# Late modulation chunks on TensorE: weight blocks stationary and one column moving, in place of a broadcast column and 512 moving

## The chip, the cores and the metric

One core of one Trainium2 chip runs the kernel. The time is the device time of one execution in microseconds (us). All data is fp32.

## The reference, cut to what matters

Two transformer blocks of two layers each work on 256 tokens of width 1024. In the first block each layer is modulated by a vector that depends on the conditioning `c` alone:

```
c_act = jax.nn.silu(c)
for layer in range(DEPTH):
    mod = (c_act @ ada_w[layer] + ada_b[layer])[:, None, :]
    sh1, sc1, g1, sh2, sc2, g2 = jnp.split(mod, 6, axis=-1)
    h = rms_norm(x, norm1_g[layer]) * (1.0 + sc1) + sh1
    x = x + g1 * mixer(h)          # even: retention and local attention; odd: stick-breaking
    h = rms_norm(x, norm2_g[layer]) * (1.0 + sc2) + sh2
    x = x + g2 * grouped_moe(h, ...)
```

`ada_w` is 2 x 1024 x 6144, 50 MB. A vector of 1024 goes against each matrix, so each weight is used once.

## The kernel before, in words

**Chunks.** The modulation is made in 24 chunks `j` of 512 outputs, 12 a layer. With `i = j % 12`, chunks with `i // 2` of 2 or 5 are gates (`g1`, `g2`), which are wanted along a row on all partitions; the others (shifts and scales) are wanted by feature, four columns of 128. In layer 0 chunks 8 and 9 are `sc2`, 10 and 11 are `g2`; in layer 1 chunks 12 and 13 are `sh1`, 14 and 15 `sc1`. Each chunk has two tiles of 1 MB (k blocks 0 to 3 and 4 to 7 of the 1024 rows), each loaded as two transfers of 512 KB.

**The ring.** All weights pass through three slots (`weight_ring`, RING = 3). SyncE issues every load in the order of the plan (`make_plan`; `ada` and `group` on SyncE's queue). Tile n goes into the slot of tile n - 3 and waits until that one is used up: for a tile summed by VectorE until its half is summed (`ada_summed`, `free`, L574 on), for a tile that TensorE reads directly until `weights_used` is raised. So a chunk and a half is all that is loaded ahead.

**Chunks on VectorE.** 21 of 24 chunks are summed by VectorE (`ada_steps`): a scaling by `c_features` of k block 0 (L2335) and seven multiply-adds (L2342), each over 128 x 512, into an accumulator. TensorE then adds over the partitions (`modulate`): four matmuls with 128 columns of the accumulator stationary and one column of ones moving (L858), or for a gate one matmul with ones stationary and 512 columns moving (L855). In the profile each such fp32 matmul is two records. VectorE takes the result (`ada_take`): adds the bias, raises `mod_taken`, and for `i` of 3 or 9 makes gain times scale.

**Chunks on TensorE.** Chunks 10, 12 and 14 (`ADA_ON_PE`) aren't summed by VectorE. TensorE reads the weights themselves (`modulate_a0`, L875): 8 matmuls with one column of `c_features` broadcast to 128 x 128 stationary and 512 weight columns moving, accumulated in one bank, with the same row on all partitions. For chunks 12 and 14, which aren't gates, `ada_take` picks the diagonal blocks out by a multiply with the identity (L2366) and a reduce (L2368).

**Where the chunks stand.** Chunks 0 to 6 are made before and within the input projection of layer 0 (`even_in`). Chunks 7 and 8 are summed within it. Chunks 7 to 15 are handed over within the local attention of layer 0 (`attention(Pairs("a0"))`), which has four items of two heads. TensorE's step t is: score products of item t (L902), values of item t - 2 (L923), fills (`stay_busy`, L739), transposes of the probabilities of item t - 1 (L937), then `in_a0(t)`, where the calls of `modulate_a0(x)` stand. Before the attention it does `modulate_a0(0)` and `(1)`. `modulate_a0(x)` for x of 2 or more waits for `mod_taken` of the chunk two places before, whose bank (6 or 7) it takes. At t of 1 TensorE also waits for `a0_mixed` and transposes the normed retention output (L1235).

VectorE's step t is: reciprocals and scaling of the probabilities of item t - 1 (L2244, L2254), shifted scores of item t (L2263), a copy of the transposed probabilities (L2271), a split of an output (L2275), then its own `in_a0(t)`: at t of 0 the take of x = 2, the reciprocal root, the mixing (L2654, raises `a0_mixed`), and a chunk's sum; at t of 1 and 2 takes and a chunk's sum; at t of 3 and 4 one take. All engines work in program order. The calls before:

```
before t=0: PE chunks 7, 8      DVE sum 9, takes 7, 8
t=0:        PE 9, 10            DVE take 9, mixing, sum 11
t=1:        PE 11, 12           DVE takes 10, 11, sum 13
t=2:        PE 13, 14           DVE takes 12, 13, sum 15
t=3:        PE 15               DVE take 14
t=4:                            DVE take 15
```

Behind the attention TensorE waits for all takes and for the split outputs, and multiplies with `even_out` (L722 to L724), whose weights ScalarE (L1520) and VectorE (L2071) first split into a high and a low part. Then come norm, router (L1078, 16 columns moving), experts, and layer 1, where chunks 16 to 23 are summed by VectorE.

Of the kernel before, what the change touches and what calls it, by code (L numbers as in the profile page):

```python
# [8 lines left out]
ALU = mybir.AluOpType  # L9
# [24 lines left out]
PASSES = GROUPS  # L34

ADA_EVEN, ADA_A0, ADA_ODD, ADA_A1 = (0, 1, 4, 5, 6, 6), 6, 4, 4
ADA_ON_PE = (10, 12, 14)
EVEN_ORDER = [0, 1, 4, 5, 2, 6, 3]
PASS_TILES = 6 * PER_GROUP
EV_ORDER = [3, 4, 5, 0, 1, 2]  # L40
# [63 lines left out]
def make_plan():  # L104

    p = Plan()
    st = {"ada": []}

    def group(name, evac, width=512):

        ts = p.tiles_of(2)
        for t in ts:
            p.tiles[t]["size"] = 4 * width
        st.setdefault(name, []).append((ts, [p.chunk(ts[1], tb == 1, evac) for tb in range(TB)]))

    def proj(name, cols, evac):
        for j in range(-(-cols // 512)):
            group(name, evac, min(512, cols - 512 * j))

    def ada(count):  # L120
        for _ in range(count):
            kind = dict(user="pe", split=False) if len(st["ada"]) in ADA_ON_PE else dict(user="ada")
            st["ada"].append(p.tiles_of(2, **kind))

    def experts(l):
        st[f"moe{l}"] = p.tiles_of(PASSES * PASS_TILES)[0]

    def feed_forward(l):
        st[f"ffn{l}"] = p.tiles_of(3 * FFN_STEPS)[0]
        p.evac["dve"] += 4  # L130

    def cross(l):
        t = p.tile()
        st[f"caq{l}"] = (t, [p.chunk(t, i == 1, "act") for i in range(2)])
        t = p.tile()
        st[f"cao{l}"] = (t, [p.chunk(t, i == 3, "dve") for i in range(4)])

    for l in range(2):
        p.turn(f"mem{l}", KD)
        st[f"kv{l}"] = []  # L140
        for _ in range(2):
            ada(1)
            st[f"kv{l}"].append([p.chunk(None, False, "act") for i in range(2)])
    p.turn("a0h1", KD)
    for j in range(7):
        group("even_in", "act")
        ada(ADA_EVEN.count(j))
    ada(ADA_A0)
    proj("even_out", D, "dve")
    p.turn("a0h2", KD)  # L150
    experts(0)
    p.turn("a1h1", KD)
    for j in range(6):
        group("odd_in", "act")
        if 1 <= j <= ADA_ODD:
            ada(1)
    p.turn("a1qk", 16)
    ada(ADA_A1)
    proj("odd_out", D, "dve")
    p.turn("a1h2", KD)  # L160
    experts(1)
    for j in EV_ORDER:
        if j == EV_ORDER[-1]:
            st["cmp"] = p.tiles_of(2, split=False)
        group("ev_in", "act", min(512, EV_IN - 512 * j))
    p.turn("b0sparse", 8)
    p.turn("b0forget", 8)
    proj("ev_out", D, "dve")
    cross(0)
    feed_forward(0)  # L170
    proj("od_in", OD_IN, "act")
    p.turn("b1q", 8)
    p.turn("b1k", 8)
    proj("od_out", D, "dve")
    cross(1)
    feed_forward(1)
    assert len(st["ada"]) == 24
    return p, st


def build(nc, a, out):
# [3 lines left out]
    with ctx:  # L185
# [85 lines left out]
        PS = ctx.enter_context(nc.psum_tensor("banks", [128, 8, 512], F32))  # L271
        B = [PS[:, i, :] for i in range(8)]

        ADA_ON_DVE = [j for j in range(24) if j not in ADA_ON_PE]

        def ada_sum(j):

# [91 lines left out]
        def slot(n):  # L369
            return W[:, n % RING, :]  # L370
# [175 lines left out]
        def _(eng):  # L546
# [28 lines left out]

            def ada(count=1):
                for _ in range(count):
                    j = loaded_chunks[0]
                    loaded_chunks[0] += 1
                    group(st["ada"][j], a["ada_w"][j // 12], 512 * (j % 12))  # L580

# [118 lines left out]
        def _(eng):  # L700
# [160 lines left out]

            def modulate_a0(x):

                j, bank = 7 + x, 6 + x % 2
                if x >= 2:
                    eng.wait_ge(mod_taken, 7 + x - 1)
                if j not in ADA_ON_PE:
                    modulate(j, bank)
                    return
                for i, t in enumerate(st["ada"][j]):  # L870
                    loaded(t)
                    w = slot(t).rearrange("p (k n) -> p k n", k=4)
                    for k in range(4):
                        at = 4 * i + k
                        mm = eng.matmul(B[bank][:, :], CF[:, at:at + 1].to_broadcast([128, 128]), w[:, k, :],  # L875
                                        start=at == 0, stop=at == KD - 1)
                    mm.then_inc(*used.up())

            normed_n = [0]

# [342 lines left out]
            def in_a0(t):  # L1223

                if t == 0:
                    modulate_a0(2)
                    modulate_a0(3)
                if t == 1:
                    modulate_a0(4)
                    eng.wait_ge(a0_mixed, 1)  # L1230
                    for k in range(RET_HEADS):
                        for tb in range(TB):
# [2 lines left out]
                            mm = eng.transpose(B[2 + k // 2][:, at:at + 128], block, by)  # L1235
                        if k % 2:
                            mm.then_inc(feature_turned, 2)
                    modulate_a0(5)
                    features_wait(RET_HEADS)
                if t == 2:  # L1240
                    modulate_a0(6)
                    modulate_a0(7)
                if t == 3:
                    modulate_a0(8)
            attention(Pairs("a0", P0), in_a0)
            ada[0] += 3 + ADA_A0
            eng.wait_ge(mod_taken, 16)
# [804 lines left out]
        def _(eng):  # L2052
# [292 lines left out]

            ada_taken = [0]

            def ada_take(j, banks, room=None):

                l, i = j // 12, j % 12  # L2350
                if j == 16:
# [7 lines left out]
                if i // 2 in (2, 5):  # L2359
                    g = GB[:, int(i // 2 == 5), (i % 2) * 512:(i % 2 + 1) * 512]  # L2360
                    V(g, bank[:, :], g, ALU.add).then_inc(mod_taken, 1)
                else:
                    new = bank[:, 0:4]
                    if j in ADA_ON_PE:
                        rows = lambda ap: ap.rearrange("p (i f) -> p i f", i=4)
                        V(rows(room), rows(bank), wide(ident.unsqueeze(1), 128, 4, 128), ALU.mult).then_inc(*vec.up())  # L2366
                        settle()
                        eng.tensor_reduce(to, rows(room), AX.X, ALU.add).then_inc(*vec.up())  # L2368
                        settle()
                        new = to  # L2370
                    V(to, new, ABF[:, l, 4 * i:4 * i + 4], ALU.add).then_inc(mod_taken, 1)  # L2371
                if i in (3, 9):
                    n = 2 * l + i // 6
                    eng.wait_ge(mod_taken, ada_taken[0])
# [259 lines left out]
                eng.wait_ge(ret_scores, h + 1)  # L2634
                V(SCR[:, h, :], B[(2, 3, 0, 1)[h]][:, 0:384], SCR[:, h, :], ALU.mult).then_inc(ret_decayed, 1)
            eng.wait_ge(bias_masked, 1)
            room = P0[:, 0, 512:1024]

            def take_a0(x):
                ada_take(7 + x, (6 + x % 2,), room)  # L2640
            ada_steps(KD)
            take_a0(0)
            take_a0(1)

            def in_a0(t):
# [11 lines left out]
                    ins.then_inc(a0_mixed, 1)  # L2657
                    ada_steps(KD)
                if t == 1:
                    take_a0(3)  # L2660
                    for i in range(2):
                        parts[0] += 2
                        eng.wait_ge(features_high, parts[0])
                        hl, hh = [ap[:, 2 * i:2 * i + 2, :].rearrange("p k n -> p (k n)") for ap in (HL, HH)]
                        V(hl, B[2 + i][:, :], hh.bitcast(F32), ALU.subtract).then_inc(features_split, 2)
                    take_a0(4)
                    ada_steps(KD)
                if t == 2:
                    take_a0(5)
                    take_a0(6)  # L2670
                    ada_steps(KD)
                if t == 3:
                    take_a0(7)
                if t == 4:
                    take_a0(8)
            attention(Pairs("a0", P0), (), in_a0)
            splits(at_split[0] + 2)
            add_projected("even_out", 0)
# [425 lines left out]
```

## Time and profile before

| | us |
|---|---|
| median of 3 runs | 1932.01 |
| lowest, highest | 1924.81, 1933.83 |
| profiled execution, its own time | 1938.03 |
| its span | 1936.2 |
| mean granted TensorE clock | 0.962 of 2.4 GHz |

The profile is of one execution; its span runs from the first to the last instruction, and 1.8 us of its own time lie around it. TensorE (PE) has the matmuls, PEld its weight loads, DVE is VectorE, ACT ScalarE, SPq the DMA queue of SyncE. A row of the timeline gives the start, the time from the first start to the last end of a run of like instructions, and in brackets the idle time of the engine before it and what ended it. The clock is given as a share of 2.4 GHz; 0.50 is 1.2 GHz.

### The profile page before, as it was taken

The page shows a single profiled execution, that of the slowest core. Times are in us where ns is not written, and L with a number is a line of the kernel's source. Part 1 is how long each engine was busy: PE and PEld are TensorE (multiplying, and loading weights), DVE is VectorE, ACT ScalarE, POOL GpSimd, SP SyncE. Part 2 cuts the span into 40 slices and gives each one's busy share as a digit, 9 for nine tenths or more (in the row PEclk, how much of TensorE's full clock was granted, in tenths as well). Part 3 has the DMA queues.
Part 4 walks back from the last instruction along what each step waited for, and adds up shares of the span by engine and source line. Part 5 has one row for each costly group of instructions (what it writes and reads, how often), then busy time and mean ns, then how long its engine had stood idle before and what let it go on. Part 6 is the DMA issues. An engine that isn't in the chain of part 4 may idle for free.

```text
span 1936.2 us, 27184 instructions
## 1 busy us (share of the span) xinstructions
PE 1807.3 (93%) x9604; PEld 1494.8 (77%) x9604; DVE 1264.0 (65%) x2000; ACT 1072.8 (55%) x1649; POOL 13.8 (1%) x29
## 2 busy tenths in 40 slices
PE   5998899999999999999999999988999998889998
PEld 4785478888886866888888678676999876669997
DVE  5686658889885766589889652755544565555454
ACT  2443247878873364578878552555444454554443
POOL 1000000000000000000000000000000000000000
PEclk9998889999999999899999998889999999989999
DMA  9866638899993845399899653122656561215652
GB/s 351 298 237 228 202 125 314 323 356 357 322 352 135 314 131 174 120 352 356 324 355 355 224 158 118 44 88 66 186 184 195 166 207 54 88 44 175 194 177 85
DMA packets 217285, 413.09 MB, mean 213 GB/s; under 512 B 13120, under 2 KB 69488, under 8 KB 216800
## 3 DMA queue, kind: packets, MB, share of 16 engines
q1 hardware_dynamic: 214176, 400.74, 60.2%
q0 software_dynamic: 1904, 8.26, 1.3%
q10 hardware_dynamic: 1120, 2.97, 0.4%
q8 instruction: 52, 0.85, 0.2%
q14 instruction: 33, 0.27, 0.0%
HBM read 410.87 MB, written 1.05 MB: 213 GB/s over the span
## 4 chain that ended last, share of the span: by engine, by line
PE 80%; DVE 10%; ACT 5%; issue 2%; DMA 2%; DVEq 0%; ACTq 0%; SPq 0%
PE banks L722 21%; PE banks L724 20%; PE banks L723 20%; PE banks L739 2%; DVE weights_low L2071 2%; PE banks L984 2%; PE banks L1126 2%; DMA weight_ring<-in_ada_w 2%; PE banks L1069 1%; DVE row_gains L2342 1%; PE banks L752 1%; ACT scratch L1671 1%; PE banks L923 1%; PE banks L779 1%; PE banks L875 1%
## 5 line engine op out<-in xcount | busy, mean ns | idle before, releaser
L2071 DVE TENSOR_TENSOR weights_low<-weight_ring,weights_high 128x1024 fp32r<-128x1024 f32 (+1 forms) x656 | 771.8, 1218 | 186.7 <-ACT weights_high L1520 106.5
L722 PE MATMUL banks<-weights_high,features_parts 128*128 128x512 f32 (+1 forms) x1488 | 590.8, 397 | 19.4 <-DVE features_parts L2504 8.2
L724 PE MATMUL banks<-weights_high,features_parts 128*128 128x512 f32 (+1 forms) x1488 | 581.1, 391 | 0.0
L723 PE MATMUL banks<-weights_low,features_parts 128*128 128x512 f32 (+1 forms) x1488 | 581.0, 390 | 0.0
L1800 ACT ACTIVATE weights_high<-weight_ring 128x1024 fp32r<-128x1024 f32 x384 | 391.1, 1055 | 102.4 <-PE banks L724 72.7
L722 PEld LDWEIGHTS banks<-weights_high,features_parts 128*128 128x128 f32 x1488 | 281.3, 189 | 84.4 <-DVE weights_low L2071 16.3
L724 PEld LDWEIGHTS banks<-weights_high,features_parts 128*128 128x128 f32 x1488 | 280.9, 189 | 59.4
L723 PEld LDWEIGHTS banks<-weights_low,features_parts 128*128 128x128 f32 x1488 | 281.2, 189 | 55.4 <-issue 1.0
L1520 ACT ACTIVATE weights_high<-weight_ring 128x1024 fp32r<-128x1024 f32 (+1 forms) x176 | 176.0, 1043 | 139.3 <-PE banks L724 85.5
L722 PE MATMUL banks<-features_parts,weights_high 128*128 128x256 f32 x736 | 210.5, 286 | 1.1 <-DVE features_parts L2166 1.0
L723 PE MATMUL banks<-features_parts,weights_high 128*128 128x256 f32 x736 | 208.4, 283 | 0.0
L724 PE MATMUL banks<-features_parts,weights_low 128*128 128x256 f32 x736 | 208.4, 283 | 0.0
L722 PEld LDWEIGHTS banks<-features_parts,weights_high 128*128 128x128 f32 x736 | 141.3, 192 | 3.2 <-issue 1.7
L723 PEld LDWEIGHTS banks<-features_parts,weights_high 128*128 128x128 f32 x736 | 141.5, 192 | 0.7
L724 PEld LDWEIGHTS banks<-features_parts,weights_low 128*128 128x128 f32 x736 | 141.3, 192 | 0.0
L2016 ACT ACTIVATE weights_high<-weight_ring 128x1024 fp32r<-128x1024 f32 x96 | 96.0, 1048 | 55.8 <-PE banks L724 55.8
L739 PE MATMUL banks<-fill 128*128 128x512 f32 x406 | 124.0, 450 | 0.3 <-DVE modulation L2371 0.3
L2342 DVE SCALAR_TENSOR_TENSOR row_gains<-weight_ring,c_features,row_gains 128x512 f32<-128x512 f32 x133 | 99.9, 751 | 28.6 <-DMA weight_ring<-in_ada_w 20.8
L739 PEld LDWEIGHTS banks<-fill 128*128 128x128 f32 x406 | 82.9, 214 | 23.7 <-issue 8.1
L2903 DVE TENSOR_TENSOR projected<-projected,banks 128x256 f32<-128x256 f32 x44 | 18.5, 421 | 104.6 <-PE banks L724 104.6
L1671 ACT ACTIVATE scratch<-scratch,row_shifts 128x128 f32<-128x128 f32 (+1 forms) x80 | 36.2, 454 | 71.6 <-DVE row_shifts L2263 71.6
L1993 ACT ACTIVATE features_parts<-projected 128x512 fp32r<-128x512 f32 x22 | 13.9, 630 | 74.7 <-PE banks L724 74.7
(371 smaller groups left out, 1620.2 us busy)
## 6 DMA issues: line engine op xcount, KB each, us to landing
weight_ring<-in_exp_w_gate SPq DMA_DIRECT2D x128, 512.0 KB, 5.0
weight_ring<-in_exp_w_up SPq DMA_DIRECT2D x128, 512.0 KB, 5.0
weight_ring<-in_exp_w_down SPq DMA_DIRECT2D x128, 512.0 KB, 5.1
weight_ring<-in_ada_w SPq DMA_DIRECT2D x96, 512.0 KB, 5.6
weight_ring<-in_ffn_wg SPq DMA_DIRECT2D x44, 512.0 KB, 4.1
weight_ring<-in_ffn_wu SPq DMA_DIRECT2D x44, 512.0 KB, 4.7
weight_ring<-in_ffn_wd SPq DMA_DIRECT2D x44, 512.0 KB, 4.2
weight_ring<-in_even_w_in SPq DMA_DIRECT2D x28, 512.0 KB, 5.7
```

Source lines behind the costliest of these rows:

```text
L722: eng.matmul(dst, lh, rh, start=first, stop=False, **kw)
L723: eng.matmul(dst, lh, rl, start=False, stop=False, **kw)
L724: mm = eng.matmul(dst, ll, rh, start=False, stop=last, **kw)
L739: eng.matmul(B[bank][:, :], FILL[:, :], FILL[:, :].unsqueeze(1).to_broadcast([128, 4, 128]), start=True, stop=True, skip_group_check=True)
L984: mm = eng.matmul(B[4 + b][:, k * 128:(k + 1) * 128], NB[:, tb, (4 * b + k) * 128:(4 * b + k + 1) * 128], SEL[:, tb, :], start=(tb == 0), ...
L1126: mm = eng.matmul(B[4 + q % 4][:, 0:256], left, right, start=i == 0, stop=i == len(steps) - 1)
L1520: eng.activation(half_of(high(s), i, t["size"]), half_of(slot(t["n"]), i, t["size"]), ACT.Copy)\
L1671: eng.activation(p, p, ACT.Exp, scale=-1.0, bias=small(SHIFT, t)[:, i:i + 1], accum_out=small(SUMS, t)[:, i:i + 1]).then_inc(probs_ready, 1)
L1800: eng.activation(half_of(high(t["split"]), x), half_of(slot(t["n"]), x), ACT.Copy)\
L2016: eng.activation(half_of(high(t["split"]), x), half_of(slot(t["n"]), x), ACT.Copy)\
L2071: V(half_of(low(s), i, size), half_of(slot(n), i, size), half_of(high(s), i, size).bitcast(F32), ALU.subtract)\
L2342: ins = eng.scalar_tensor_tensor(out=acc, in0=w, scalar=CF[:, k:k + 1], in1=acc, op0=ALU.mult, op1=ALU.add)
```

## The change

Of chunks 7 to 15, TensorE now makes 9, 12, 13, 14 and 15 from the weights, none of them a gate; the gates 10 and 11 are summed by VectorE. TensorE's form is turned round: a block of 128 x 128 weights is stationary and one column of `c_features` moves, 32 matmuls a chunk (for each of four blocks of outputs, eight of k), and the result stands by feature in four columns. TensorE waits for both tiles before the first matmul, and the first tile is given back only four matmuls (eight records) before the last (`i == 3`, `k == 3`), the second at the last. Chunk 12 is loaded ahead of 11 (`ADA_LOADS`). `ada_take` needs no identity and no reduce. The calls of both engines move:

```
before t=0: PE chunks 7, 8      DVE takes 7, 8
t=0:        PE 9                DVE take 9, mixing, sum 10
t=1:        PE 10, 12           DVE take 10, sum 11
t=2:        PE 11, 13           DVE takes 12, 11
t=3:        PE 14               DVE take 13
t=4:        PE 15               DVE take 14
t=5:                            DVE take 15
```

The diff, cut to its core:

```diff
-ADA_ON_PE = (10, 12, 14)
+ADA_ON_PE = (9, 12, 13, 14, 15)
+ADA_LOADS = [*range(11), 12, 11, *range(13, 24)]
+A0_CHUNKS = [7, 8, *ADA_LOADS[9:16]]
...
     def ada(count):
         for _ in range(count):
-            kind = dict(user="pe", split=False) if len(st["ada"]) in ADA_ON_PE else dict(user="ada")
-            st["ada"].append(p.tiles_of(2, **kind))
+            j = ADA_LOADS[len(st["ada"])]
+            kind = dict(user="pe", split=False) if j in ADA_ON_PE else dict(user="ada")
+            st["ada"][j] = p.tiles_of(2, **kind)
...
             def modulate_a0(x):
 
-                j, bank = 7 + x, 6 + x % 2
+                j, bank = A0_CHUNKS[x], 6 + x % 2
...
-                for i, t in enumerate(st["ada"][j]):
+                for t in st["ada"][j]:
                     loaded(t)
-                    w = slot(t).rearrange("p (k n) -> p k n", k=4)
-                    for k in range(4):
-                        at = 4 * i + k
-                        mm = eng.matmul(B[bank][:, :], CF[:, at:at + 1].to_broadcast([128, 128]), w[:, k, :],
-                                        start=at == 0, stop=at == KD - 1)
-                    mm.then_inc(*used.up())
+                for i in range(4):
+                    for k in range(KD):
+                        w = slot(st["ada"][j][k // 4]).rearrange("p (k n) -> p k n", k=4)[:, k % 4]
+                        mm = eng.matmul(B[bank][:, i:i + 1], w[:, i * 128:(i + 1) * 128], CF[:, k:k + 1],
+                                        start=k == 0, stop=k == KD - 1)
+                        if i == 3 and k % 4 == 3:
+                            mm.then_inc(*used.up())
...
                 if t == 0:
                     modulate_a0(2)
-                    modulate_a0(3)
                 if t == 1:
-                    modulate_a0(4)
                     eng.wait_ge(a0_mixed, 1)
...
-                    modulate_a0(5)
+                    modulate_a0(3)
+                    modulate_a0(4)
                     features_wait(RET_HEADS)
                 if t == 2:
+                    modulate_a0(5)
                     modulate_a0(6)
-                    modulate_a0(7)
-                if t == 3:
-                    modulate_a0(8)
+                if t in (3, 4):
+                    modulate_a0(t + 4)
...
-                    new = bank[:, 0:4]
-                    if j in ADA_ON_PE:
-                        rows = lambda ap: ap.rearrange("p (i f) -> p i f", i=4)
-                        V(rows(room), rows(bank), wide(ident.unsqueeze(1), 128, 4, 128), ALU.mult).then_inc(*vec.up())
-                        settle()
-                        eng.tensor_reduce(to, rows(room), AX.X, ALU.add).then_inc(*vec.up())
-                        settle()
-                        new = to
-                    V(to, new, ABF[:, l, 4 * i:4 * i + 4], ALU.add).then_inc(mod_taken, 1)
+                    V(to, bank[:, 0:4], ABF[:, l, 4 * i:4 * i + 4], ALU.add).then_inc(mod_taken, 1)
...
-            ada_steps(KD)
             take_a0(0)
             take_a0(1)
...
                 if t == 1:
-                    take_a0(3)
...
-                    take_a0(4)
+                    take_a0(3)
                     ada_steps(KD)
                 if t == 2:
+                    take_a0(4)
                     take_a0(5)
-                    take_a0(6)
-                    ada_steps(KD)
-                if t == 3:
-                    take_a0(7)
-                if t == 4:
-                    take_a0(8)
+                if 3 <= t <= 5:
+                    take_a0(t + 3)
```

## Rows read from the trace of the kernel before

**Rows 1.** The page: busy time, clock in 40 slices, the chain that ended last.

```profile
PE 1807.3 (93%) x9604; PEld 1494.8 (77%) x9604; DVE 1264.0 (65%) x2000; ACT 1072.8 (55%) x1649; POOL 13.8 (1%) x29
...
PEclk9998889999999999899999998889999999989999
...
PE 80%; DVE 10%; ACT 5%; issue 2%; DMA 2%; DVEq 0%; ACTq 0%; SPq 0%
```

**Rows 2.** Waits from 110 to 260 us: total, times, longest (us).

```profile
ACT scratch L1671 <- DVE row_shifts L2263: 45.0, 4, 15.1
...
DVE row_gains L2342 <- DMA weight_ring<-in_ada_w: 12.4, 4, 4.9
```

**Rows 3.** Timeline of TensorE, 155 to 236 us: start, duration (us), instruction, idle before.

```profile
164.78 1.84 PE L858 MATMUL banks<-constants,row_gains 128*128 128x1 f32 x16
166.56 0.93 PE L902 MATMUL banks<-qk_features 64*128 64x128 f32 x8
172.22 1.84 PE L858 MATMUL banks<-constants,row_gains 128*128 128x1 f32 x8 [4.73 <-DVE modulation L2371]
173.92 10.03 PE L875 MATMUL banks<-weight_ring,c_features 128*128 128x512 f32 x16
...
188.39 1.54 PE L937 MATMUL banks<-constants,scratch 128*128 128x128 f32 x6 [3.59 <-DVE scratch L2254]
189.73 1.92 PE L855 MATMUL banks<-row_gains,constants 128*128 128x512 f32 x2
191.44 1.91 PE L1235 MATMUL banks<-constants,normed 128*128 128x128 f32 x8
193.14 7.19 PE L875 MATMUL banks<-weight_ring,c_features 128*128 128x512 f32 x16
...
205.17 1.00 PE L937 MATMUL banks<-constants,scratch 128*128 128x128 f32 x6 [2.29 <-DVE scratch L2254]
...
208.72 9.71 PE L875 MATMUL banks<-weight_ring,c_features 128*128 128x512 f32 x16 [1.76 <-DVE modulation L2371]
...
227.14 1.65 PE L739 MATMUL banks<-fill 128*128 128x512 f32 x3
...
231.14 1.55 PE L923 MATMUL banks<-scratch,projected 128*64 128x256 f32 x8 [1.07 <-DVE features_parts L2275]
232.62 2.94 PE L739 MATMUL banks<-fill 128*128 128x512 f32 x8
```

**Rows 4.** Stretches: us; busy by engine (instructions); clock; DMA share; GB/s.

```profile
168.00:172.00 4.00, 0.00 (x0) 0.00 (x0) 3.69 (x6) 1.04 (x1) 0.00 (x0) 0.69 0.77 217
194.00:197.00 3.00, 3.00 (x8) 1.33 (x7) 2.71 (x5) 0.04 (x1) 0.00 (x0) 1.00 0.03 6
266.00:268.00 2.00, 1.60 (x15) 1.63 (x15) 0.25 (x1) 1.34 (x2) 0.00 (x0) 1.00 0.00 0
270.00:272.00 2.00, 2.00 (x11) 2.00 (x11) 0.00 (x0) 0.00 (x0) 0.00 (x0) 0.50 0.00 0
```

**Rows 5.** Timeline of VectorE in the same stage.

```profile
165.87 0.49 DVE L2335 TENSOR_SCALAR row_gains<-weight_ring,c_features 128x512 f32<-128x512 f32 x1 [8.51 <-PE banks L858]
166.39 5.68 DVE L2342 SCALAR_TENSOR_TENSOR row_gains<-weight_ring,c_features,row_gains 128x512 f32<-128x512 f32 x7
...
174.61 2.16 DVE L2654 SCALAR_TENSOR_TENSOR normed<-banks,reciprocal_root,projected 128x128 f32<-128x128 f32 x8
...
184.48 3.18 DVE L2342 SCALAR_TENSOR_TENSOR row_gains<-weight_ring,c_features,row_gains 128x512 f32<-128x512 f32 x4 [4.89 <-DMA weight_ring<-in_ada_w]
...
207.78 0.69 DVE L2368 TENSOR_REDUCE modulation<-projected 128x4 f32<-128x512 f32 x1
```

**Rows 6.** Timeline of TensorE at the router's products, 253 to 292 us.

```profile
266.40 1.93 PE L1078 MATMUL banks<-router_w,qk_features 128*128 128x16 f32 x16 [0.73 <-DVE qk_features L2105]
...
269.71 3.43 PE L1078 MATMUL banks<-router_w,qk_features 128*128 128x16 f32 x16
```

**Rows 7.** Timeline of the DMA issues on SyncE's queue, 180 to 183 us.

```profile
180.55 0.88 SPq L563 DMA_DIRECT2D weight_ring<-in_ada_w  x2
```

More of the change, by code:

```diff
@@ L106, in make_plan @@
     p = Plan()
-    st = {"ada": []}
+    st = {"ada": {}}
     def group(name, evac, width=512):
@@ L272, in build @@
         B = [PS[:, i, :] for i in range(8)]
-        ADA_ON_DVE = [j for j in range(24) if j not in ADA_ON_PE]
+        ADA_ON_DVE = [j for j in ADA_LOADS if j not in ADA_ON_PE]
         def ada_sum(j):
@@ L577, in ada @@
                 for _ in range(count):
-                    j = loaded_chunks[0]
+                    j = ADA_LOADS[loaded_chunks[0]]
                     loaded_chunks[0] += 1
@@ L2346, in _, with ada_take @@
             ada_taken = [0]
-            def ada_take(j, banks, room=None):
+            def ada_take(j, banks):
                 l, i = j // 12, j % 12
@@ L2636, in _ @@
             eng.wait_ge(bias_masked, 1)
-            room = P0[:, 0, 512:1024]
             def take_a0(x):
-                ada_take(7 + x, (6 + x % 2,), room)
-            ada_steps(KD)
+                ada_take(A0_CHUNKS[x], (6 + x % 2,))
             take_a0(0)
```

## The prediction

> **What bounds the kernel now.** I read the page first: TensorE is busy 93% of the span at a granted clock mostly of 2.4 GHz, and the chain that ended last lies on it for 80% [rows 1]. That average hides the stage of the change, the local attention of layer 0 (165 to 236 us), so I then read the waits of that stretch. ScalarE's exponentials wait 45.0 us in four waits on VectorE, and VectorE's chunk sums wait 12.4 us for transfers [rows 2]. The timeline of TensorE shows the stage as a chain in program order: score products, transposes of the last item, chunks between them, with TensorE idle before several pieces [rows 3]. So the end of the stage is set by TensorE and VectorE in turn. Whatever stands between two items on TensorE is on the path; its gaps (4.73, 3.59, 2.29, 1.76 us) are what could cover new work. The clock matters here as nowhere else: 0.69 of full over 168 to 172 us, 1.00 at 194 to 197 [rows 4].
>
> **What the change removes.** VectorE sums 19 chunks and not 21. In the stage it summed 9, 11, 13 and 15; now 10 and 11. A chunk is one scaling and seven multiply-adds, 0.49 + 5.68, back to back 6.1 us [rows 5], so 12.3 us go. The multiply by the identity and the reduce of the old TensorE chunks 12 and 14 (the reduce alone 0.69 us, twice) go too [rows 5]. TensorE loses three chunks of 16 records of 512 columns: 10.03, 7.19 and 9.71 us, 27 us in all [rows 3]; also three small column sums (1.84 us at the low clock, about 0.95 at the high).
>
> **What it adds.** Five chunks, each of 32 fp32 matmuls. The column sum L858 is the same form (128x128 stationary, one column moving); its 16 records stand for 8 matmuls, so a chunk is 64 records. Price at 2.4 GHz: 16 records took 1.84 us [rows 3], 0.106 each, 6.9 us a chunk. Price at 1.2 GHz: eight records at 172.22 took 1.84 us, 0.213 each, 13.8 us a chunk. No row shows 64 in a run, so these are the two ends. The old chunk took 7.2 us at the high clock, so at the high clock a chunk costs what it did, and at the low clock a third more than the 10.03 of the slowest old one.
>
> **Which end.** The router's products are the nearest row: 16 columns moving, 32 records in two groups of 16 [rows 6]. The first 16 took 1.93 us; the clock fell with TensorE hardly idle (1.60 us busy in 266 to 268, then 2.00 in 270 to 272 at 0.50), and the next 16 took 3.43 us [rows 4, 6]. Half the records at each price gives 32 x 0.106 + 32 x 0.213 = 10.2, with the last one's end 10.3 us a chunk. I take that for the four chunks that follow dense work (transposes, fills, scores), which raised the clock before them: at 194 to 197 it was back at 1.00 after the 128- and 512-column work from 188.39 on [rows 3, 4].
>
> The Trainium skill, "TensorE: Matmul & The Clock Gate", section "Why this matters for your kernels", says to keep TensorE continuously busy and free of long idle gaps, and the clock stays released. Taken by itself that would give the new chunks the 2.4 GHz price, since they leave no gap, and the first rival's time below. The router rows speak against it.
>
> **The sum along the path**, in the profile's own times.
> - Chunk 9. TensorE needn't wait for VectorE's sum of it (the 4.73 us idle before 172.22 goes), and starts at 167.4. Until then it does what it did, so the clock falls at about 169.5 as before [rows 4]: 20 records at 0.106, 44 at 0.213, end 179.1.
> - VectorE takes it only then, and the mixing (2.16 us [rows 5]) stands behind that take: 181.8. Chunk 10's sum, 6.1 us, to 188.0; its second tile lands before it is wanted (its slot is free at 177.4, and 3.9 us pass from issue to use, as from 180.55 to 184.48 [rows 5, 7]). The transposes start at 188.8, not 188.39: +0.4. So what VectorE gains by not summing chunk 9 is spent waiting for it.
> - Transposes, normed transposes and chunk 10's ones-matmul, issued 1.3 + 1.7 + 1.7 us [rows 3], to 193.6. Chunk 12: 203.9 (its old end was 200.3): +3.6.
> - The second tile of chunk 11 is behind chunk 12 in the ring: its slot comes free 8 records before the end of chunk 12, at 202.2, lands at 206.1, four steps take 3.2 us (as from 184.48) and scaling 0.9: transposes at 210.2, not 205.17: +5.0. The reorder 12, 11 doesn't remove this wait, it makes it hang on a longer chunk.
> - 1.4 + 1.7 us, then chunk 13: 223.6. Its old counterpart, chunk 14, ended at 218.4: +5.2.
> - From here VectorE sums nothing and the old waits are gone, but TensorE is back to back: scores 1.8, values 1.5, fills 1.6, transposes 1.4 (low-clock rows [rows 3]; scores twice their 0.93) to 229.9; chunk 14 to 240.2; 4.5 us more to 244.7; chunk 15 to 255.0. Then the last values, which stood at 231.14.
>
> That is **+23.9 us**. The transfers of 14, 15 and of the second tile of even_out come free at 221.9, 238.5 and 253.3 and land 3.9 us later, before 229.9, 244.7 and the 259 at which ScalarE reaches that tile: hidden by 4.1, 2.3 and about 1.5 us; without that cover each costs its lateness. The swap of loads 11 and 12, the new bank order and the extra step of takes cost nothing besides: the moved instructions (0.15 to 0.7 us) lie in VectorE's waits. Behind the last values nothing changes: fills, splits and even_out follow as from 232.62 on.
>
> The profiled execution's time is 1938.0 us (span 1936.2), 6.0 above the median 1932.0 of the runs. 1938.0 + 23.9 = 1961.9; on the median, 1932.0 + 24 = **1956 us**.
>
> **Rivals.**
> 1. *The high clock holds* (not slower). Chunk 9 ends at 174.3, VectorE's chunk 10 at 183.1, transposes 183.9; chunk 12 at 193.4; chunk 11's late tile lands 196.5, transposes 200.6; chunks 13, 14, 15 end at 209.2, 219.7 and 230.1, the last two each after 3.9 us for a tile behind the chunk before. Last values at 230.1 and not 231.14: -1 us, 1931. It decides if a chunk runs at 0.106 throughout. For it: L858 in pairs at the high clock. Against: the router's records. Chance 0.12, with anything up to +9.
> 2. *The low clock throughout.* Four chunks at 13.8 and not 10.3 add 14 us: +38, 1970. For it: the clock stayed low through L858 and the first matmuls after it (172.22 to 178). Against: 5 to 6 us of dense work between chunks. A tile landing late adds to it. Chance 0.17 for +31 and more.
> 3. *VectorE was the bound and TensorE's gaps take the work.* At the high clock five chunks are 34.5 us against 21.6 + 2.9 before, 10 us more, while the five gaps of [rows 3] hold 13.4, and the old chunks' low-clock share (27 - 21.6 = 5 us) is saved: -11, 1921. Against: gaps aren't where the chunks stand; VectorE now waits for chunk 9, and two late tiles remain. Chance 0.05.
>
> **Chances and range.** The forecast's own case, a chunk of 9.5 to 11.7 us, holds +20 to +31 us, 1952 to 1963, with 0.62; 0.04 lies between it and the first rival. A measurement can tell some 0.5%, 9.7 us, from no change: faster 0.05, same 0.12, slower 0.83. The range 1944 to 1969 leaves out the first and third rival and the worst of the second.
>
> **What would show it.** Right: the new chunk matmuls with 64 records each, single records spaced 0.106 in a first part and 0.213 after; the clock at 0.50 for most of 170 to 255 us, with the low digit in two more slices of the page; VectorE idle 5 us or more before the take of chunk 9, and again for chunk 11's second tile; the last values near 255; everything behind shifted alike. Wrong: clock at 1.00 in the middle of a chunk's second half (first rival); no gap on VectorE before the mixing; a TensorE wait for a tile above 1 us; or a shift that shrinks after even_out.

## The result, and the profile after

The changed kernel takes 1959.2 us in the median of 4 runs (1952.2 to 1963.5), the kernel before 1930.1 in the same comparison: ratio 1.0142, 95% interval [1.0112, 1.0172]. A second comparison of the unedited changed kernel (6 runs, below) gave 1.0168 [1.0143, 1.0193]. The profiled execution took 1963.5 us, with a span of 1961.8.

Three lines of the page, against [rows 1]: TensorE is busier by 32 us, its clock shows 7 and 5 tenths in the fourth and fifth slice, where 8 and 8 stood before, and it holds one more per cent of the chain.

```profile
PE 1839.2 (94%) x9854; PEld 1542.0 (79%) x9854; DVE 1251.0 (64%) x1980; ACT 1074.0 (55%) x1649; POOL 13.8 (1%) x29
...
PEclk9997589999999999899999998798999998989999
...
PE 81%; DVE 9%; ACT 5%; issue 2%; DMA 1%; SPq 0%; DVEq 0%; ACTq 0%
```

The timeline of TensorE in the stage, against [rows 3]. L878 is the new chunk line, L906 the scores, L927 the values, L941 the transposes, L742 the fills; the five rows of L878 are chunks 9, 12, 13, 14 and 15.

```profile
164.54 0.93 PE L906 MATMUL banks<-qk_features 64*128 64x128 f32 x8
165.40 11.54 PE L878 MATMUL banks<-c_features,weight_ring 128*128 128x1 f32 x64
...
186.48 1.54 PE L941 MATMUL banks<-constants,scratch 128*128 128x128 f32 x6 [7.97 <-DVE scratch L2257]
...
191.23 10.55 PE L878 MATMUL banks<-c_features,weight_ring 128*128 128x1 f32 x64
...
208.07 1.06 PE L941 MATMUL banks<-constants,scratch 128*128 128x128 f32 x6 [2.04 <-DVE scratch L2257]
...
211.82 13.79 PE L878 MATMUL banks<-c_features,weight_ring 128*128 128x1 f32 x64 [0.98 <-DMA weight_ring<-in_ada_w]
...
230.39 11.47 PE L878 MATMUL banks<-c_features,weight_ring 128*128 128x1 f32 x64
...
245.98 10.55 PE L878 MATMUL banks<-c_features,weight_ring 128*128 128x1 f32 x64
256.46 1.55 PE L927 MATMUL banks<-scratch,projected 128*64 128x256 f32 x8
```

Both stages are best measured from the start of the first score products to the start of the last values: 64.6 us before (166.56 to 231.14), 91.9 now (164.54 to 256.46), **27.3 us more**. In front of it this execution was 2.0 us earlier, behind it both take the same, 1705.1 and 1705.3 us to the end of the span: 27.3 - 2.0 + 0.3 is the span's 25.6. So between these two executions the stage is the whole difference.

The new chunks take 11.54, 10.55, 13.79, 11.47 and 10.55 us, 57.9 in all. The clock over six stretches (columns as in [rows 4]): in chunks 12 and 14 it is high in the first microseconds and low in the rest, in chunk 13 low from the start, while TensorE is busy without a gap.

```profile
192.00:195.00 3.00, 3.00 (x29) 3.00 (x29) 2.81 (x5) 0.00 (x0) 0.00 (x0) 1.00 0.00 0
196.00:201.00 5.00, 5.00 (x26) 5.00 (x25) 0.00 (x0) 0.00 (x0) 0.00 (x0) 0.50 0.00 0
...
206.00:208.00 2.00, 0.04 (x1) 0.00 (x0) 1.93 (x6) 0.00 (x0) 0.00 (x0) 1.00 1.02 368
...
212.00:225.00 13.00, 13.00 (x62) 13.00 (x63) 0.70 (x3) 0.00 (x0) 0.00 (x0) 0.50 0.10 36
231.00:233.00 2.00, 2.00 (x20) 2.00 (x19) 1.64 (x8) 0.03 (x1) 0.00 (x0) 0.95 0.44 164
234.00:241.00 7.00, 7.00 (x34) 7.00 (x34) 0.00 (x0) 0.00 (x0) 0.00 (x0) 0.50 0.00 0
```

Single records of chunk 9 in two stretches, 165 to 167 us and 170 to 176 us (duration in ns, least/median/most):

```profile
L878 PE MATMUL banks<-c_features,weight_ring x15: 250/250/271, 165.4 to 167.0; 128*128 128x1 f32 x15
```

```profile
L878 PE MATMUL banks<-c_features,weight_ring x30: 352/352/352, 169.8 to 175.9; 128*128 128x1 f32 x30
```

15 records start within 1.6 us at the high clock and 30 within 6.1 us at the low: 0.11 us apart, and 0.21.

VectorE, against [rows 5], now waits where it worked before: 10.27 us for chunk 9, 9.17 us for the second tile of chunk 11, 14.52 us for scores behind chunk 13.

```profile
176.97 0.16 DVE L2366 TENSOR_TENSOR modulation<-banks,ada_bias_features 128x4 f32<-128x4 f32 x1 [10.27 <-PE banks L878]
...
204.16 3.18 DVE L2345 SCALAR_TENSOR_TENSOR row_gains<-weight_ring,c_features,row_gains 128x512 f32<-128x512 f32 x4 [9.17 <-DMA weight_ring<-in_ada_w]
...
227.22 0.29 DVE L2266 CUSTOM_DVE_ANT_0 scratch<-banks,aux 128x128 f32<-128x128 f32 x1 [14.52 <-PE banks L906]
```

### The profile page after: what moved, and what is told of

Its sections match the earlier page's. It is cut to its first block, busy times and chain, and to the rows that moved or that the text cites. A ratio compares the mean times of both kernels' runs of the same rounds, so it can differ in the third digit from the quotient of the medians.

```text
span 1961.8 us, 27659 instructions
## 1 busy us (share of the span) xinstructions
PE 1839.2 (94%) x9854; PEld 1542.0 (79%) x9854; DVE 1251.0 (64%) x1980; ACT 1074.0 (55%) x1649; POOL 13.8 (1%) x29
## 4 chain that ended last, share of the span: by engine, by line
PE 81%; DVE 9%; ACT 5%; issue 2%; DMA 1%; SPq 0%; DVEq 0%; ACTq 0%
PE banks L725 21%; PE banks L727 20%; PE banks L726 20%; PE banks L878 3%; DVE weights_low L2074 2%; PE banks L742 2%; PE banks L988 2%; PE banks L1130 1%; PE banks L1073 1%; DMA weight_ring<-in_ada_w 1%; DVE row_gains L2345 1%; PE banks L755 1%; PE banks L782 1%; PE banks L906 1%; PE banks L927 1%
## 5 line engine op out<-in xcount | busy, mean ns | idle before, releaser
L742 PE MATMUL banks<-fill 128*128 128x512 f32 x406 | 121.6, 444 | 0.3 <-DVE modulation L2366 0.3
L2345 DVE SCALAR_TENSOR_TENSOR row_gains<-weight_ring,c_features,row_gains 128x512 f32<-128x512 f32 x119 | 89.4, 751 | 24.8 <-DMA weight_ring<-in_ada_w 17.5
L742 PEld LDWEIGHTS banks<-fill 128*128 128x128 f32 x406 | 81.7, 211 | 23.4 <-issue 8.0
L878 PEld LDWEIGHTS banks<-c_features,weight_ring 128*128 128x128 f32 x320 | 58.1, 286 | 3.9 <-DVE row_gains L2364 2.5
```

The costliest lines, as they stand in the source:

```text
L742: eng.matmul(B[bank][:, :], FILL[:, :], FILL[:, :].unsqueeze(1).to_broadcast([128, 4, 128]), start=True, stop=True, skip_group_check=True)
L878: mm = eng.matmul(B[bank][:, i:i + 1], w[:, i * 128:(i + 1) * 128], CF[:, k:k + 1], start=k == 0, stop=k == KD - 1)
L2345: ins = eng.scalar_tensor_tensor(out=acc, in0=w, scalar=CF[:, k:k + 1], in1=acc, op0=ALU.mult, op1=ALU.add)
```

## The experiments

Ratios are to the kernel before, run on the same chip. "Stage" is the time from the first scores to the last values in the one profiled execution of each version, and line numbers shift by a few from version to version. The rest of the kernel is the same in all versions, yet from the last values to the end of the span the profiled executions took from 1690 to 1708 us, and the stage of one and the same version moved by 3.8 us (run 10). So neither a span nor a few microseconds of one stage tell versions apart by themselves.

Where the rest differs, the traces show. From 940 to 1100 us behind the last values the clock was 0.82 to 0.85 in the five executions whose rest took 1704 to 1708 us (before, changed, runs 4, 8 and 10), 0.91 to 0.94 in the six with 1690 to 1694 (runs 1, 2, 5, 6, 7 and 9), and 0.88 in run 3 with 1698. The changed kernel, then run 6, over the same stretch:

```profile
1196.00:1356.00 160.00, 145.43 (x804) 112.65 (x803) 84.78 (x290) 72.38 (x201) 0.00 (x0) 0.82 0.24 79
```

```profile
1196.00:1356.00 160.00, 140.31 (x863) 107.94 (x862) 93.13 (x313) 81.16 (x226) 0.00 (x0) 0.94 0.25 80
```

Between the same two groups of transposes (L782) around that stretch, at 1138.03 and 1323.99 us in the changed kernel and at 1135.59 and 1311.36 in run 6, lie 186.0 and 175.8 us: 10 of the 13.7 us by which these two rests differ. So some 10 us of a median's difference can come from far behind the stage. Whether a version sets them or chance does, no run here shows.

**1. The same records, with 128 columns moving.** Only the moving column is repeated; the four results stand 128 columns apart.

```diff
-mm = eng.matmul(B[bank][:, i:i + 1], w[:, i * 128:(i + 1) * 128], CF[:, k:k + 1], ...)
+mm = eng.matmul(B[bank][:, i * 128:(i + 1) * 128], w[:, i * 128:(i + 1) * 128],
+                CF[:, k:k + 1].to_broadcast([128, 128]), ...)
...
-V(to, bank[:, 0:4], ABF[:, l, 4 * i:4 * i + 4], ALU.add)
+new = bank[:, 0:512:128] if j in ADA_ON_PE else bank[:, 0:4]
+V(to, new, ABF[:, l, 4 * i:4 * i + 4], ALU.add)
```

> The changed kernel, but the moving column of c_features is broadcast to 128 columns, so each of the 64 records of a chunk streams 128 columns (the normed transposes, of that width, stand 0.106 apart at 2.4 GHz and 0.213 at 1.2). Same results, same records, same weights loaded, same order; only the array is fed for the whole record. Theory (the clock falls because the matmuls are narrow): records 0.107 us apart, a chunk 6.9 us after the clock is back, clock at 1.00 through chunks 13 to 15, last values 20 to 26 us earlier than in the changed kernel; 1930 to 1938 us, ratio to the kernel before 1.000 to 1.004. Rival (64 weight loads, or the order of the chunks and their waits, set the loss, whatever the clock): chunks stay at 10.5 to 13.8 us, ratio 1.012 to 1.017.

Measured: ratio 1.0041 [1.0015, 1.0067], stage 72.8 us. Timeline of TensorE, then the clock over the last three chunks:

```profile
166.51 0.93 PE L906 MATMUL banks<-qk_features 64*128 64x128 f32 x8
167.36 7.41 PE L878 MATMUL banks<-c_features,weight_ring 128*128 128x128 f32 x64
...
189.07 7.95 PE L878 MATMUL banks<-c_features,weight_ring 128*128 128x128 f32 x64
...
203.88 1.42 PE L941 MATMUL banks<-constants,scratch 128*128 128x128 f32 x6 [4.31 <-DVE scratch L2257]
...
208.31 7.38 PE L878 MATMUL banks<-c_features,weight_ring 128*128 128x128 f32 x64 [1.30 <-DMA weight_ring<-in_ada_w]
...
220.31 7.38 PE L878 MATMUL banks<-c_features,weight_ring 128*128 128x128 f32 x64 [1.41 <-DMA weight_ring<-in_ada_w]
...
239.28 0.87 PE L927 MATMUL banks<-scratch,projected 128*64 128x256 f32 x8
```

```profile
208.00:240.00 32.00, 28.35 (x242) 26.05 (x242) 5.73 (x26) 3.27 (x12) 0.00 (x0) 1.00 0.42 145
```

The same 64 weight loads and 64 matmuls, each with 128 times the columns, take 7.4 us (chunk 12, which began at the low clock, 7.95) and not 10.5 to 13.8, and the clock stays at 1.00 through chunks 13 to 15. The stage loses 19.1 us of the 27.3, a little under the 20 to 26 expected, and the ratio is just above its range. The rival (weight loads, order, waits at whatever clock) falls. The chunk is 0.5 us longer than I expected, and the 8.2 us left are not the clock's in the main. Run 3, below, has the same order and a stage 8.0 us shorter: 4.0 us of that are waits (here 4.31 us before the second transposes, 203.88, and 1.30, 1.41 and 1.93 us for late tiles), 2.2 us the chunks' own time.

**2. The new form alone.** The kernel before, with the new form in chunks 12 and 14 and no pick by VectorE; all else as before.

```diff
+if j != 10:
+    ...                      # the 32 matmuls with one column moving
+    return
```

> The kernel before with the new form for chunks 12 and 14 alone (chunk 10, a gate, keeps its form; allocation, load order and calls are those of before). Theory (clock): chunk 12 takes 10.3 instead of 7.2 us, chunk 14 10.3 to 13.8 instead of 9.7, both on the path, less 1.4 us for the pick that goes from VectorE once before a wait of TensorE: +3 to +6 us, ratio 1.0015 to 1.003. Rival (the loss comes from the allocation and the order, not from the form): -1 to -3 us.

Measured: ratio 1.0054 [1.0034, 1.0074], stage 78.7 us (+14.1). Timeline of TensorE, the two chunks between first scores and last values:

```profile
163.12 0.93 PE L913 MATMUL banks<-qk_features 64*128 64x128 f32 x8
...
188.73 13.78 PE L876 MATMUL banks<-c_features,weight_ring 128*128 128x1 f32 x64 [0.16 <-DMA weight_ring<-in_ada_w]
...
213.60 13.78 PE L876 MATMUL banks<-c_features,weight_ring 128*128 128x1 f32 x64 [2.79 <-DMA weight_ring<-in_ada_w]
...
241.84 0.87 PE L934 MATMUL banks<-scratch,projected 128*64 128x256 f32 x8 [1.07 <-DVE features_parts L2286]
```

The sign is the theory's, the size above it: both chunks ran at the low clock from end to end, 13.78 us each, where 7.19 and 9.71 stood, and chunk 14 waited 2.79 us for its tile. Two such chunks in the old order already cost 8.8 us between the medians, where 3 to 6 were expected.

**3. The new allocation and order alone**, with the old form and VectorE's picks for all five chunks.

```diff
 ADA_ON_PE = (9, 12, 13, 14, 15)
...
-    (32 matmuls, one column moving)
+    (8 matmuls, one column broadcast and stationary, 512 moving; identity and reduce in ada_take)
```

> The changed kernel's allocation, load order and calls, with the old form of the TensorE chunks (one broadcast column stationary, 512 columns moving, and VectorE picking the diagonals). Theory (clock): each of the five chunks takes 7.2 us at the high clock and 10 to 13 at the low, which lasts only until the first dense stretch is over, so 7.2 to 10 each; against the changed kernel 5 x 2 to 3 us less, against the one before +8 to +15 us, ratio 1.004 to 1.008. Rival (the loss is in the number of chunks on TensorE, whatever the form): ratio 1.012 to 1.016.

Measured: ratio 1.0022 [0.9994, 1.0051], stage 64.8 us, against 64.6 before. Timeline of TensorE:

```profile
163.33 0.93 PE L905 MATMUL banks<-qk_features 64*128 64x128 f32 x8
...
186.77 7.03 PE L878 MATMUL banks<-weight_ring,c_features 128*128 128x512 f32 x16
...
198.19 1.00 PE L940 MATMUL banks<-constants,scratch 128*128 128x128 f32 x6 [1.84 <-DVE scratch L2256]
...
228.09 0.87 PE L926 MATMUL banks<-scratch,projected 128*64 128x256 f32 x8
```

My expectation was too high: the chunks took 7.03 to 7.13 us, all at the high clock, and their first tile comes back at half, so the second transposes waited only 1.84 us (198.19). Five chunks on TensorE and the new order cost nothing measurable. **The form is the loss, not the allocation.** Run 2 has the new form without the new allocation and order and is slower; run 3 has these without the form and isn't. To the form belongs here, beside the one moving column, that both tiles are awaited first and the first is given back late.

**4. 64 columns moving.** Run 1 with half the width; the four results stand 64 columns apart.

```diff
-CF[:, k:k + 1].to_broadcast([128, 128])
+CF[:, k:k + 1].to_broadcast([128, 64])
```

> As the run with 128 broadcast columns, with 64: the array is fed for half of each record. Theory (clock, by how wide the matmuls are): between the changed kernel and the run with 128 columns, the clock at 1.00 for more of the stage than with one column; ratio 1.002 to 1.012. If the clock acted on or off by the mere presence of one-column matmuls it would equal the run with 128 columns. Rival (weight loads): ratio 1.012 to 1.017 as changed.

Measured: ratio 1.0111 [1.0055, 1.0166] from 4 runs, stage 75.2 us. Timeline of TensorE, and the clock over chunk 14:

```profile
168.83 0.93 PE L906 MATMUL banks<-qk_features 64*128 64x128 f32 x8
...
208.90 7.39 PE L878 MATMUL banks<-c_features,weight_ring 128*128 128x64 f32 x64
...
220.87 12.16 PE L878 MATMUL banks<-c_features,weight_ring 128*128 128x64 f32 x64 [1.37 <-DMA weight_ring<-in_ada_w]
...
243.98 0.87 PE L927 MATMUL banks<-scratch,projected 128*64 128x256 f32 x8
```

```profile
221.00:232.00 11.00, 11.00 (x61) 11.00 (x61) 0.62 (x3) 0.00 (x0) 0.00 (x0) 0.58 0.16 60
```

Four of the chunks took 7.3 to 7.6 us, chunk 14 12.16, since the clock fell early within it (0.58 over 221 to 232). The stage lies between one column (91.9) and 128 (72.8). The runs of this version spread from 1937 to 1964 us, so the ratio says little more than that. No other width was tried.

**5. The first tile given back at half a chunk.** The first tile's k blocks for all four output blocks, then the second tile's. Each output block still opened its own accumulation, and the kernel's results came out wrong (run 9 has them right); instructions and transfers are as many as in the changed kernel, so the times can be compared.

```diff
-for i in range(4):
-    for k in range(KD):
+for h in range(2):
+    for i in range(4):
+        for k in range(4 * h, 4 * h + 4):
             ...
+    mm.then_inc(*used.up())
```

> The changed kernel with the 64 records of a chunk in another order: the first tile's four k blocks for all four output blocks, then the second tile's. The first tile is given back after half the chunk and not 8 records before its end. Theory (the late tile of chunk 11 is a second, small loss): it comes 24 records earlier, 5.1 us at the low clock, so TensorE's 2.04 us before the transposes and 0.98 us before chunk 13 go: 3 us less than the changed kernel, ratio 1.012 to 1.013; the chunks' own 10.5 to 13.8 us stay. Rival (tiles are the main loss, not the clock): 10 us less or more, ratio under 1.009.

Measured: ratio 1.0130 [1.0102, 1.0158], stage 89.9 us, 2.0 less than the changed kernel. Timeline of TensorE:

```profile
167.27 0.93 PE L906 MATMUL banks<-qk_features 64*128 64x128 f32 x8
...
208.61 0.82 PE L941 MATMUL banks<-constants,scratch 128*128 128x128 f32 x6
...
213.68 12.66 PE L879 MATMUL banks<-c_features,weight_ring 128*128 128x1 f32 x64 [3.39 <-DMA weight_ring<-in_ada_w]
...
257.17 1.55 PE L927 MATMUL banks<-scratch,projected 128*64 128x256 f32 x8
```

The 2.04 us before the second transposes are gone (208.61 follows the fills), but chunk 13's own second tile is late by 3.39 us in their place, where it was 0.98. So the waits together are no shorter, and of the 2.0 us 1.4 are the chunks' own (56.5 us in all, not 57.9), which move by more than that between executions of one version (run 10). The early return alone has no gain that can be told; the rival (10 us) falls.

**6. VectorE takes chunk 9 later**, behind the mixing and the sum of chunk 10.

```diff
 if t == 0:
-    take_a0(2)
     root(8)
     ...
     ada_steps(KD)
+    take_a0(2)
```

> The changed kernel, but VectorE takes chunk 9 behind the mixing and the sum of chunk 10, not ahead of them. Theory: mixing and the first tile's steps go into the 10.3 us in which VectorE waited for chunk 9; the second tile of chunk 10 (issued 176.0, lands 180) and its four steps then set the transposes at 184 and not 186.5: 2.5 us less than the changed kernel, ratio 1.0125 to 1.0135. Rival (VectorE isn't on the path there): no difference.

Measured: ratio 1.0095 [1.0069, 1.0120], stage 90.2 us, 1.7 less than the changed kernel. Timeline of VectorE at chunk 10's second tile:

```profile
181.35 1.54 DVE L2345 SCALAR_TENSOR_TENSOR row_gains<-weight_ring,c_features,row_gains 128x512 f32<-128x512 f32 x2 [8.53 <-DMA weight_ring<-in_ada_w]
```

VectorE is on the path there: TensorE's idle time before the first transposes is 4.99 us and not 7.97. VectorE now waits for the tile that TensorE's chunk 9 holds. Chunk 9 took 12.89 us in this execution and not 11.54, so its tile came back 1.35 us later; that covers the 0.8 us missing from the 2.5 expected. The 1.7 us by themselves lie within what one version's stage moves by; run 8 against run 3 tests the same edit with chunks whose times hardly change. The ratio is lower than the stage explains: against the 1.0142 and 1.0168 of the changed kernel it says 9 to 14 us. The difference lies behind the stage: the rest took 1691.6 us here and 1705.3 and 1703.6 in the two profiles of the changed kernel, at the clocks shown above. Why stays open.

**7. All three together**: 128 columns, first tile back at half, later take. The results are wrong as in run 5, the instructions the same in number and size.

> The changed kernel with the 128 broadcast columns, the first tile given back at half, and the take of chunk 9 behind the sum of chunk 10. Theory: the three losses are the clock, the late tiles and the take, and they are all of it. Against the run with 128 columns alone: transposes of item 0 5.4 us earlier, 3.1 of the 4.3 us before the next ones gone, and the 1.30, 1.41 and 1.93 us for tiles gone, so the last values come 59 us after the first scores (before 64.6, changed 91.9): 1924 to 1926 us, ratio 0.996 to 0.999. Rival (something else holds the stage): ratio 1.001 to 1.004.

Measured: ratio 0.9946 [0.9927, 0.9966], stage 60.1 us, 31.8 less than the changed kernel: the three losses together are more than the 27.3 us, and nothing else holds the stage. The ratio is below its range of 0.996 to 0.999. It says 10 us against the kernel before, the stage 4.5; the rest took 1692.0 us here and 1705.1 in the profile of before.

**8. The old form in the new order, with the later take.**

> The allocation and order of the changed kernel with the old form (512 columns moving), and the take of chunk 9 behind the sum of chunk 10. Theory: as the run of that order with the old form, whose last values came 64.8 us after the first scores, less the 5.8 us by which the mixing and the sum of chunk 10 come earlier: 59 us, ratio 0.997 to 1.000. Rival: no difference from the old form in that order, 1.002.

Measured: ratio 0.9966 [0.9946, 0.9987], stage 60.2 us, 4.6 less than run 3. The chunks took 7.03 to 7.18 us in both runs, and TensorE's idle time before the first transposes went from 10.13 to 5.21 us, so these 4.6 us are the later take's. The ratio is just below its range. It is faster than the kernel before, by 0.3%; its rest (1705.2 us) was as long as that of before (1705.1), and the stage is 4.4 us shorter.

**9. Run 7 with one opening a chunk.**

```diff
-start=k == 0, stop=k == KD - 1, skip_group_check=True)
+start=h == i == k == 0, stop=k == KD - 1, skip_group_check=True)
```

> As the run with 128 columns, the first tile given back at half and the later take, but only the first matmul of a chunk opens an accumulation, not the first of each of the four output blocks. With four openings the first tile's share was lost from the sums. Theory: an opening clears the accumulate marks of the whole bank, so the three later openings made the second tile's matmuls overwrite what the first had left in the blocks before; with one opening nothing is lost. The instructions are the same in number and size, so the time is that of the run with four: last values 60 us after the first scores, 1922 us, ratio 0.993 to 0.997. Rival (the loss of the sums has another cause, or an opening costs time): sums still off, or another time.

Measured: the sums are whole; ratio 0.9976 [0.9954, 0.9998], stage 62.7 us. Timeline of TensorE:

```profile
165.24 0.93 PE L906 MATMUL banks<-qk_features 64*128 64x128 f32 x8
...
178.45 1.40 PE L941 MATMUL banks<-constants,scratch 128*128 128x128 f32 x6 [4.08 <-DVE scratch L2257]
...
199.18 8.98 PE L879 MATMUL banks<-c_features,weight_ring 128*128 128x128 f32 x64 [0.75 <-DVE row_gains L2364]
...
227.95 0.87 PE L927 MATMUL banks<-scratch,projected 128*64 128x256 f32 x8
```

The time is 2.6 us longer in the stage than run 7's, of which chunk 13 is 1.6 (8.98 and not 7.38 us: it began at the low clock, 0.50 over 199 to 201). That is within what the stage moves by between executions. The ratio is a little above its range; it is under 1 by hardly more than its interval, and the stage is 1.9 us shorter than before. Between runs 7, 8 and 9 the intervals overlap; I would take run 8, whose chunks are the shorter.

**10. The changed kernel again.**

> The changed kernel itself, unedited, against the kernel before, beside the version above on the same chip. Theory: the stage takes 90 to 93 us from the first scores to the last values against 64.6, so +26 to +28 us; ratio 1.012 to 1.016. If the later take and the early return of tiles (each 1.7 to 2.0 us shorter in the stage, but 1.0095 and 1.0130 as ratios) had gained more than their stages show, it stays at 1.014; if those ratios scatter by what the rest of the kernel does, it may come out lower, at 1.010 to 1.013.

Measured: ratio 1.0168 [1.0143, 1.0193], just above the range; stage 95.7 us, also above it. Timeline of TensorE:

```profile
212.74 12.85 PE L878 MATMUL banks<-c_features,weight_ring 128*128 128x1 f32 x64 [2.47 <-DMA weight_ring<-in_ada_w]
```

Chunks 12.71, 11.40, 12.85, 10.77 and 13.65 us: the last one never saw the high clock for long. The same program's stage differs by 3.8 us between the two profiled executions, and 3.5 of these are the chunks', by where in each the clock falls. The wait for chunk 13's tile was 2.47 us here and 0.98 there.

## Why the prediction was right

It forecast 1956 us with a range of 1944 to 1969, slower; 1959.2 was measured. The case that came true is the forecast's own, +20 to +31 us, but at its upper end: the medians lie 29.1 us apart and not 24, and part of the nearness is that the kernel before came out at 1930.1, 2 us under the median it was added to. In run 10 the ratio says 32 us, in the second rival's band. Step by step, with the execution's times moved by the 2.0 us by which its first scores came earlier:

- *Chunk 9* was to end at 179.1 and ended at 179.0; *the transposes of item 0* 188.8 and 188.5; *chunk 12* 203.9 and 203.8; *the transposes of item 1*, behind the late tile, 210.2 and 210.1. So for these steps the two prices per record (0.106 and 0.213), the shares at either (20 and 44 records in chunk 9, half and half in chunk 12), the take of chunk 9 ahead of the mixing, and the ring's wait behind chunk 12 are right to 0.3 us. That is of this execution: in run 10 chunk 9 took 12.71 us and chunk 12 11.40, each about 1 us more.
- *Chunk 13* was to end at 223.6 and ended at 227.6. Here the size is off by 4.0 us: the middle price of 10.3 us was taken for every chunk that follows dense work, and this one took 13.79, the low price. The clock had risen by 206 (1.00 in the stretch 206 to 208) but TensorE stood idle for 2.04 us there and again for 0.98 us, and it was down again before the chunk. Those 0.98 us, for the chunk's own second tile, the sum had at nothing; a tile wait above 1 us was among its signs of being wrong, and in run 10 this one was 2.47 us. It is the second rival's price in one of four chunks, and in run 10 chunk 15 took nearly that price too (13.65). Over both profiled executions the eight chunks behind dense work average 11.9 us, so the middle price was too low, not only unlucky once.
- *Chunks 14 and 15* took 11.47 and 10.55 us, and from the end of 13 to the last values I had 31.4 and measured 30.9. That is in part luck: the two chunks were together 1.4 us longer than twice 10.3, and the work before them 1.9 us shorter than its low-clock prices (4.8 and 4.1 us, not 6.3 and 4.5), the first mostly since the clock rose there (L742 1.30 us, L941 0.82). The sum came to +23.9, the stage to +27.3: the 3.4 us are chunk 13's.
- *What VectorE sheds* buys nothing: VectorE does 12.3 us less of sums and stands in the waits of 10.27, 9.17 and 14.52 us shown above. That the first of them was on the path, run 6 and run 8 against run 3 show; for the others it is read from the timeline.
- *The reason for the low clock.* The router's records were the evidence, and run 1 is the test: equal records with wider moving operand, 19 us back. The first rival needed the high clock all through a chunk of one-column matmuls; none of the ten such chunks profiled in the two executions of the changed kernel had it (10.55 us was the shortest, 6.9 its price). The Trainium skill, "TensorE: Matmul & The Clock Gate", section "Why this matters for your kernels", advises keeping TensorE continuously busy. By this case that isn't enough: 13.00 of 13 us busy over 212 to 225 at a clock of 0.50, and 28.35 of 32 us busy at 1.00 with 128 columns. The measurement decides.
- *The third rival* (VectorE was the bound, 1921 us) was wrong for this change. Its own terms (10 us more, less 13.4 and 5) come to some -8 us, not the -11 that it states. Runs 7 and 8, at 1922 and 1924 us, are near its number, but their stages are 4.5 and 4.4 us shorter than before, not 11. So much the gaps could take once the chunks ran at the high clock and VectorE no longer waited for chunk 9.

What I expected wrongly in the experiments was twice the same thing: the chance share of the low clock, taken as a middle price where an execution has one end or the other (runs 2 and 3). Beside these, the ratios of runs 1, 7, 8, 9 and 10 lay outside their ranges by 0.0001 to 0.0014, that of run 6 by 0.003; that is no more than the stage and the rest move by between executions.

## What to carry to other kernels

Don't price a long run of narrow matmuls at the high clock: with one column moving, the weights stationary and TensorE always busy, 64 records took 10.5 to 13.8 us here, and with 128 equal columns mostly 7.4. The added columns cost some 0.5 us a chunk against the 6.9 that one column would take at the high clock, and over the last three chunks the clock stood at 1.00. And a take that waits for a long chunk belongs behind everything on its engine that doesn't need it: that was worth 4.6 us in the stage (run 8 against run 3). Before a few microseconds are put down to a change, look where in the trace two executions differ.

## What the runs showed of the hardware that was not expected

- A wider moving operand made the same work faster: 7.4 us against 10.5 to 13.8 for 64 fp32 records of a 128x128 weight block, 128 columns against one.
- Opening an accumulation in one column block of a PSUM bank acted on the blocks beside it. With the four blocks of a bank each opened (start set) and continued later, the results came out wrong; with only the first matmul of the bank opening, the same order of matmuls gave right ones (runs 5, 7 and 9). The Trainium skill, "PSUM — Partial Sum Buffer", section "The four PSUM rules", states it so: a group's first matmul clears the accumulate bits of the whole bank it touches, and a second group opened beside it makes the first one's next matmul overwrite. The runs agree with it: wrong results with four openings, right ones with one.
- From the last values to the end, the same work took 1690 to 1708 us in twelve profiled executions, and the time went with the clock in one stretch a millisecond behind the stage: 0.82 to 0.85 in the five longest, 0.91 to 0.94 in the six shortest.
